# Attention pipeline of a two-stack transformer kernel: reciprocals one step later, weights in place, ScalarE copies between exponentials, compressed softmax spread over six steps

## What is computed

```python
def first_block(x, ...):
    for layer in range(DEPTH):                      # two layers
        h = rms_norm(x, attn_norm[layer])
        if layer % 2 == 0:                          # "layer 0"
            a_out = nsa_attention(...)              # compressed + selected + window branch, gated
            b_out = swa_sink_attention(...)         # sliding window with a sink
            x = x + jnp.concatenate([a_out, b_out], axis=-1) @ w_out_e[i]
        else:                                       # "layer 1"
            x = x + dilated_attention(...) @ w_out_o[j]
        x = x + (jax.nn.silu(gate) * up) @ w_down[layer]

def second_block(x, mem, ...):
    for layer in range(DEPTH):
        y = fox_shortconv_mixer(...) if layer % 2 == 0 else rglru_mixer(...)  # the first has a
        ...                                                # forgetting attention, 8 heads
        y = memory_cross_attention(h, m, ...)       # 4 heads of 256, 256 memory tokens
        ...
        y = swiglu(h, w_ffn_gu[layer], w_ffn_down[layer])

# each attention, per head and block of 128 queries:
s = q @ k.T * scale + mask;  p = softmax(s);  out = p @ v
```

## Time and profile before

| | |
|---|---|
| Runs | 3107.08, 3118.51, 3129.29 us; median 3118.51 |
| The profiled execution | 3109.32 us, of which 3107.5 us are the span from first to last instruction |
| Granted TensorE clock, mean | 0.958 |
| Busy share | PE 91%, DVE 36%, ACT 35%, POOL 42% |
| Chain that ended last | PE 81%, DVE 11%, ACT 4%, issue 3% |

### The profile page before, as it was taken

The page is one execution under the profiler, slowest core; times in us unless marked ns, Lnnn a source line. Parts: engine busy times, 40 slices in busy tenths (PEclk is TensorE's granted clock), DMA queues, the critical chain, the costliest instruction groups (busy, mean ns, idle before and its releaser), DMA issues.

```text
span 3107.5 us, 37798 instructions
## 1 busy us (share of the span) xinstructions
PE 2832.7 (91%) x13318; PEld 2229.3 (72%) x13318; DVE 1122.2 (36%) x1969; ACT 1089.1 (35%) x1761; POOL 1315.0 (42%) x691
## 2 busy tenths in 40 slices
PE   7977999999978999989988998999978689799997
PEld 5745788887746788867757876888856577588885
DVE  5554322112553322033446325221074573432202
ACT  5654322223654322232243333222225343332221
POOL 4544444444464444434344533444423364244442
PEclk9999999999999999989989998999988899899998
DMA  4300322333201333322203311223312231122331
GB/s 153 109 2 15 95 91 92 96 103 95 94 1 58 95 94 94 98 78 82 88 21 95 115 55 61 91 91 102 101 47 75 81 123 54 54 95 94 94 97 59
DMA packets 69090, 251.77 MB, mean 81 GB/s; under 512 B 7672, under 2 KB 7928, under 8 KB 68736
## 3 DMA queue, kind: packets, MB, share of 16 engines
q1 hardware_dynamic: 67104, 244.35, 24.9%
q10 hardware_dynamic: 1888, 6.14, 0.5%
HBM read 248.36 MB, written 2.10 MB: 81 GB/s over the span
## 4 chain that ended last, share of the span: by engine, by line
PE 81%; DVE 11%; ACT 4%; issue 3%; DMA 0%; ACTq 0%; POOL 0%; DVEq 0%; POOLq 0%
PE ps L512 25%; PE ps L513 24%; PE ps L514 24%; PE ps L622 3%; ACT pr L949 2%; PE ps L607 2%; PE ps L637 1%; DVE acc L1229 1%; DVE xl L1236 1%; DVE rstd L1250 1%; ACT pt L958 1%; DVE x L1509 1%; DVE y_mid L1508 1%; PE ps L578 1%; DVE u_r L1633 1%
## 5 line engine op out<-in xcount | busy, mean ns | idle before, releaser
L449 POOL TENSOR_TENSOR w_lo<-w_raw,w_hi 128x1024 fp32r<-128x1024 f32 x462 | 1117.5, 2422 | 1559.1 <-ACT w_hi L894 1549.6
L512 PE MATMUL ps<-xh,w_hi 128*128 128x512 f32 x2384 | 969.5, 407 | 85.3 <-DVE xl L1236 74.4
L513 PE MATMUL ps<-xl,w_hi 128*128 128x512 f32 x2384 | 960.2, 403 | 0.0
L514 PE MATMUL ps<-xh,w_lo 128*128 128x512 f32 x2384 | 945.4, 397 | 0.0
L894 ACT ACTIVATE w_hi<-w_raw 128x1024 fp32r<-128x1024 f32 x462 | 485.0, 1053 | 590.4 <-PE ps L514 589.7
L512 PEld LDWEIGHTS ps<-xh,w_hi 128*128 128x128 f32 x2384 | 451.8, 190 | 230.8 <-issue 70.6
L514 PEld LDWEIGHTS ps<-xh,w_lo 128*128 128x128 f32 x2384 | 454.4, 191 | 114.4
L513 PEld LDWEIGHTS ps<-xl,w_hi 128*128 128x128 f32 x2384 | 454.3, 191 | 103.1 <-issue 2.9
L512 PE MATMUL ps<-hh,w_hi 128*128 128x512 f32 x704 | 278.4, 396 | 0.0
L513 PE MATMUL ps<-hl,w_hi 128*128 128x512 f32 x704 | 278.4, 396 | 0.0
L514 PE MATMUL ps<-hh,w_lo 128*128 128x512 f32 x704 | 278.4, 395 | 0.0
(11 more groups left out here) (234 smaller groups left out, 2928.6 us busy)
## 6 DMA issues: line engine op xcount, KB each, us to landing
w_raw<-weights_in SPq DMA_DIRECT2D x462, 512.0 KB, 3.5
x<-x_in ACTq DMA_DIRECT2D x4, 512.0 KB, 10.1
mem<-mem_in ACTq DMA_DIRECT2D x2, 1024.0 KB, 4.9
x_out<-x SPq DMA_DIRECT2D x4, 512.0 KB, 2.6
rope<-rope_in ACTq DMA_DIRECT2D x1, 512.0 KB, 11.9
tab<-tables_in ACTq DMA_DIRECT2D x2, 256.0 KB, 2.8
tab<-tables_in ACTq DMA_DIRECT2D x1, 384.0 KB, 12.2
small<-small_in ACTq DMA_DIRECT2D x1, 326.5 KB, 4.7
```

Source lines behind the costliest of these rows:

```text
L449: nc.gpsimd.tensor_tensor(w_lo[:, slot], w_raw[:, slot], w_hi.bitcast(f32)[:, slot], ALU.subtract).then_inc(lo_ready, 1)
L512: nc.tensor.matmul(dst, w_hi[:, slot, w], hi, start=first, stop=False)
L513: nc.tensor.matmul(dst, w_hi[:, slot, w], lo, start=False, stop=False)
L514: return nc.tensor.matmul(dst, w_lo[:, slot, w], hi, start=False, stop=last)
```

## The change

In all five stretches:

- `sm` is gone. VectorE writes the masked scores straight into `pr`, which now has eight buffers; exponential and scaling work in place. VectorE waits for the transposes of the step four before (`n - 7`), the exponential for no transposes.
- VectorE's reciprocal of step s moves from the end of its round s to the end of its round s+1.
- Transposes of step s come in TensorE's round s+3 and ahead of the values, which come in round s+4; before, 2 and 3. `pt` has four buffers.
- ScalarE's copy stands between the two exponentials of its round.

In U0 the compressed softmax is spread out: scores in round s, mask and maximum in s+1, exponential in s+2, sum and weights in s+3, transposes in s+4, copy in s+5, with two buffers `s_c` and a semaphore for each stage. The third and fourth start at steps 14 and 26 in place of 15 and 28. The load of `cmask` is issued by ScalarE later, after the first root, and no longer belongs to the loads that TensorE waits for at the start. Four small tensors get other places in SBUF. No instruction of arithmetic is added or removed.

```diff
-        LAG = 3
+        TURN, LAG = 3, 4
-        CMP_STEPS = [(3, 0), (0, 2), (2, 15), (1, 28)]
+        CMP_STEPS = [(3, 0), (0, 2), (2, 14), (1, 26)]
...
-        sm = place("sm", [P, 4, T], 64)
-        pr = place("pr", [P, 4, T], 72)
-        pt = place("pt", [P, 3, T], 80)
+        pr = place("pr", [P, 8, T], 64)
+        pt = place("pt", [P, 4, T], 80)
...
 TensorE, after the scores of step s, ahead of the values:
+                    if TURN <= s < len(steps) + TURN:
+                        for a, u in enumerate(steps[s - TURN]["two"]):
+                            n = 2 * (s0 + s - TURN) + a
+                            pe.wait_ge(pn_ready, n + 1)
+                            if n >= 2:
+                                pe.wait_ge(pt_copied[a], n // 2)
+                            for kb in range(u["nk"] // P):
+                                last = nc.tensor.transpose(ps[:, PT_BANKS[a], tokens(kb)],
+                                                           pr[:, n % 8, tokens(kb)], ident[:])
+                            last.then_inc(pt_ready, 1)
...
 ScalarE:
-                        if n >= 4:
-                            act.wait_ge(pt_ready, n - 3)
-                        A(pr[:, n % 4, 0:nk], sm[:, n % 4, 0:nk], ACT.Exp, scale=-1.0,
-                          bias=negm[:, slot, a:a + 1],
-                          accum_out=den[:, slot, a:a + 1]).then_inc(p_ready, 1)
...
+                    if s < len(steps):
+                        exponential(0)
+                    if TURN <= s < len(steps) + TURN:
+                        copy_turned()
+                    if s < len(steps):
+                        exponential(1)
...
 VectorE:
-                        if n >= 4:
-                            dve.wait_ge(p_ready, n - 3)
+                        if n >= 8:
+                            dve.wait_ge(pt_ready, n - 7)
...
-                    if s < len(steps):
-                        dve.wait_ge(p_ready, 2 * (s0 + s) + 2)
-                        V.reciprocal(wgt[:, slot], den[:, slot]).then_inc(wgt_ready, 1)
+                    if 1 <= s <= len(steps):
+                        dve.wait_ge(p_ready, 2 * (s0 + s))
+                        before = (slot - 1) % 4
+                        V.reciprocal(wgt[:, before], den[:, before]).then_inc(wgt_ready, 1)
...
 Hooks of the compressed branch, TensorE, ScalarE, VectorE:
-                hooks.setdefault(s + 2, []).append(cmp_transposes(i))
+                hooks.setdefault(s + 4, []).append(cmp_transposes(i))
-                hooks.setdefault(s + 2, []).append(lambda i=i: cmp_copy(i))
-                hooks.setdefault(s, []).append(lambda i=i: cmp_exp(i))
+                hooks.setdefault(s + 2, []).append(lambda i=i: cmp_exp(i))
+                hooks.setdefault(s + 5, []).append(lambda i=i: cmp_copy(i))
-                hooks.setdefault(s + 1, []).append(lambda i=i, t=t: cmp_weights(i, t))
-                hooks.setdefault(s, []).append(lambda i=i, t=t: cmp_scores(i, t))
+                hooks.setdefault(s + 3, []).append(lambda i=i, t=t: cmp_weights(i, t))
+                hooks.setdefault(s + 1, []).append(lambda i=i, t=t: cmp_scores(i, t))
```

More of the change, by code:

```diff
@@ L35 @@
 ATANH_TERMS = 9
-CONST_DMAS = 4
+CONST_DMAS = 3
 X_TOTAL = 7 * KT
@@ L131, in two_stacks @@
         rstd = sb("rstd", [P, T])
+        with ExitStack() as over_acc:
+            hid, kc_t, cmask = (over_acc.enter_context(nc.sbuf_tensor(name, shape, f32)) for name, shape in
+                                (("hid", [P, 2, 2, BLK]), ("kc_t", [P, 2, 32]), ("cmask", [P, TB, 32])))
+        with nc.sbuf_tensor("gate_t", [P, TB, 24], f32) as gate_t:
+            pass
         acc = sb("acc", [P, T])
@@ L168, in two_stacks @@
         pc_t = place("pc_t", [P, 2, 2, P], 2)
-        s_c = place("s_c", [P, 8, 32], 4)
+        s_c = place("s_c", [P, 2, 8, 32], 4)
         z_v0 = place("z_v0", [P, 3, T], 4)
@@ L629, in attention @@
                         last.then_inc(o_done, 1)
[L630 to L639, removed]
                     for hook in hooks.get(s, []):
@@ L721, in run @@
                                                 kc_t[:].rearrange("p g c -> p (g c)"), start=True, stop=True)
-                    last.then_inc(cmp_ps, 1)
+                    last.then_inc(cmp_scored, 1)
                 return run
@@ L727, in run @@
                     pe.wait_ge(cmp_norm, i + 1)
+                    if i:
+                        pe.wait_ge(cmp_copied, i)
+                    else:
+                        pe.wait_ge(cmp_masked, 2)
                     for g in range(2):
@@ L942, in attention, with exponential, copy_turned @@
                 for s in range(len(steps) + LAG):
-                    for a, u in enumerate(steps[s]["two"] if s < len(steps) else []):
-                        n, slot = 2 * (s0 + s) + a, (s0 + s) % 4
-                        nk = u["nk"] + (u["sink"] is not None)
+                    slot = (s0 + s) % 4
+                    def exponential(a):
+                        u, n = steps[s]["two"][a], 2 * (s0 + s) + a
+                        p = pr[:, n % 8, 0:u["nk"] + (u["sink"] is not None)]
                         act.wait_ge(sm_done, n + 1)
-                        if n >= 4:
-                            act.wait_ge(pt_ready, n - 3)
-                        A(pr[:, n % 4, 0:nk], sm[:, n % 4, 0:nk], ACT.Exp, scale=-1.0,
-                          bias=negm[:, slot, a:a + 1],
-                          accum_out=den[:, slot, a:a + 1]).then_inc(p_ready, 1)
[L952 to L958, removed]
+                        A(p, p, ACT.Exp, scale=-1.0, bias=negm[:, slot, a:a + 1],
+                          accum_out=den[:, slot, a:a + 1]).then_inc(p_ready, 1)
+                    def copy_turned():
+                        n = 2 * (s0 + s - TURN) + 1
+                        nk = steps[s - TURN]["two"][1]["nk"]
+                        act.wait_ge(pt_ready, n + 1)
+                        if n >= 4:
+                            act.wait_ge(o_done, (n - 3) // 2)
+                        A(pt[:, n % 4, 0:nk], ps[:, PT_BANKS[1], 0:nk], ACT.Copy).then_inc(pt_copied[1], 1)
+                    if s < len(steps):
[4 more added lines that the diff above has]
+                        exponential(1)
                     if s >= LAG and steps[s - LAG]["ends"]:
@@ L1018, in _ @@
                     root()
+                    act.dma_start(cmask[:], cmpmask_in).then_inc(cmask_in, 16)
                 if m in (10, 14):
```

64 lines of the change are left out of this document (33 added, 31 removed).

## The result

The changed kernel takes **3040.35 us** (median of four runs, 3038.09 to 3042.11), the kernel before in the same series 3114.16. The ratio is 0.9759, 95% interval 0.9727 to 0.9791. A second series gave 3041.14 against 3107.43, ratio 0.9781 (0.9768 to 0.9794). The profiled execution took 3041.29 us (span 3039.5), against 3109.32 before: 68 us less, where the sum of the prediction had 49.

What follows compares the result with a forecast made beforehand. A one-round ring of waits, exponentials on transposes, idles TensorE; cut, TensorE binds. Terms 19.8 + 21.5 + 3 + 4.6 = 49 us off 3109.3 give 3060, or 3069.5 from the median; 3066 taken, range 3042 to 3100.

Steps and rivals of the forecast that it cites:

- The ring is cut: U1: exponentials stop waiting for transposes (36.7 us); TensorE then binds at 4.6 us per pair of rounds instead of 5.90.
- the closed ring: Rival: a three-round ring through transposes, copy, exponential and GpSimd holds the round at 2.95 us; 3112 to 3118; chance 0.08.
- half the gain: Rival: GpSimd waits for the late reciprocal and TensorE for GpSimd, a pair takes 5.3 us; 26 us, 3089; chance 0.22.
- The thin margin of the late reciprocal: Transposes in round s+3 come some 0.3 us after GpSimd's scaling ends, so the reciprocal may wait a round.
- U1, 19.8 us: TensorE idling in U1 falls from 27.8 us by 19.8; 8 stay: start 5, end 1, eight splits 2.
- U0, 21.5 us: TensorE idling in U0 falls from 41.5 us by 21.5; 20 stay.
- fill 8, end and splits 4, compressed branch 8: U0's 20 us of remaining TensorE idling: pipeline start, last copy with group splits, and VectorE's compressed work for four blocks.
- UF, 3 us: TensorE idling in UF falls from 8.1 us by 3, from trailing-round holes and tenths per pair; 5 stay.
- more than the sum: Rival: UF leaves the lower clock level earlier (up to 10 us) and fills shrink; 3045; chance 0.08.
- UX, 4.6 us: The two UX together lose 4.6 us as trailing rounds lose their holes, less one copy at the end.
- The clock as a loss: Rival: U1 and the rest of UF run at the lower clock, +40 us in all, 3149; chance 0.05.
- The instructions that GpSimd lengthens: U0: eight compressed-softmax instructions slowed beside GpSimd scaling cost 1.5 us, within the branch's 8; bounds nothing to 6 us.

Runs made afterwards that it cites:

- bufs_only: Kernel before with only the eight pr buffers and in-place exponential and scaling; 3071.68 us, ratio 0.9882 to the kernel before.
- bufs_lag: Changed kernel with the reciprocal back in its own round and ScalarE's copy back behind both exponentials; 3051.87 us, ratio 0.9807 to the kernel before.
- turn2_lag3: Changed kernel with transposes two and values three rounds after the scores in U1, UF and UX, U0 unchanged; 3079.59 us, ratio 0.9889 to the kernel before.
- cmp_old: Changed kernel with the compressed softmax staged as before, its blocks at steps 2, 15 and 28 again; 3042.45 us, ratio 0.9788 to the kernel before.
- recip_own: Changed kernel with only the reciprocal back at the end of its own round; 3052.68 us, ratio 0.9815 to the kernel before.

## Why the prediction was right or wrong

The sign and the mechanism were right, the size was not: I had put 3066 us as the median, 3042 to 3100 as the range, and 3040.35 were measured. Between the two profiled executions the sum was 19 us short. The other 6 us of the miss are what I had added to 3060 for the spread of the runs.

**The ring is cut: right.** Exponentials no longer wait for transposes, TensorE binds in U1 at 4.46 us a pair, 4.8 as the mean of the four pairs with splits among them (rounds 8 to 15, 19.4 us; forecast 4.6 to 4.8), and the rivals of the closed ring and of half the gain did not come. `bufs_only` says what the prediction did not: cutting this ring alone gives about half, since a second one, values behind the copy of their block, holds most of the rest: the later rounds give about 20 us (`bufs_lag`), reciprocal and copy together the last 10. The prediction had both in its chain but counted them as one.

**The thin margin of the late reciprocal: right.** Rounds s+3 are needed, as `turn2_lag3` shows with 20.1 us of waits for GpSimd.

**U1, 19.8 us: right**, 18.5 measured. Of the 8 that were to stay 8.9 did. But the parts were off: the start has 2.5 us of holes, not 5, and the splits have the other 4.6 of the 7.1 us, not 2.

**U0, 21.5 us: the failed step**, 33.2 measured. The prediction let 20 us of idling stay: fill 8, end and splits 4, compressed branch 8. 11.5 stayed: the terms for the fill and for the branch were too large. TensorE's waits in U0:

```profile
PE ps L611 <- DVE negm L1326: 6.3, 8, 2.0
...
PE ps L726 <- DVE s_c L1466: 1.5, 1, 1.5
...
PE ps L751 <- ACT pc_t L1075: 1.0, 1, 1.0
```

With 0.9 us at the compressed transposes (L739) the compressed branch holds 3.4 us, not 8. The splits with the first minima hold 6.3. The first ten us, where I had put a fill of 8, have 2.0 us of holes, 1.5 of which are the compressed branch's. So the fill is the larger error. The kernel before had shown less than 8 there already, 4.6 us of holes in its first twelve:

```profile
146.64 2.08 PE L607 MATMUL ps<-k_r,q_r 64*128 64x512 f32 x4 [3.28 <-DVE negm L1309]
...
152.34 1.10 PE L720 MATMUL ps<-kc_t,q_p 128*128 128x64 f32 x8 [1.29 <-ACT pc_t L1058]
```

And in U1, where I had put 5, it had 3.0. In the new order TensorE has one more round of scores to do before the first transposes, which start in U0 at 147.18 and in U1 at 829.16 without a wait for GpSimd. The mistake with the branch was to charge VectorE's 3.3 us per block as if VectorE were the bound, while the same argument had TensorE bind: VectorE waits for scores for 24.4 us in U0, and extra work falls into that. `cmp_old` shows it is not the spread that saves it: staged as before, U0 is as long at full clock. The other 3 us of U0's gain are not idle time at all but busy time, 111.4 to 108.3, which the sum never held. The lower clock is part of that: U0 had 11.5 us at 0.50 before and 6.8 after, worth at most 2.4 us.

**UF, 3 us: right as idle time, wrong as length.** Idling fell by 3.3 us (6.7 to 3.4), in the second pair of profiles from 6.6 to 3.0. The length fell by 9.7 (second pair 8.6), the rest being TensorE's busy time, 58.5 to 52.1: the spell at 1.2 GHz was 10 and 17 us in place of 24. This is the rival "more than the sum", which I gave 0.08, with its mechanism (UF leaves the lower level earlier) and nearly its size. It should have had more, since that row already stood there with 12 us to win and only idle time was counted.

**UX, 4.6 us:** 5.4 measured. The trailing rounds have no hole left.

**The clock as a loss:** refuted for this kernel as a whole; U1 did fall from 0.97 to 0.93, 11.5 us at the lower level in place of 6.8, which is worth at most 2.4 us that the forecast of U1 did not hold. Why a spell ends sooner in one kernel than in another stays open. Density alone does not explain it: the changed kernel and `recip_own` have the same order of work on TensorE and nearly the same idling in UF (3 and 2.4 us), but spells of 10 and 17 against 27 us; `turn2_lag3`, whose TensorE waits more, has 34. For the rule on transposes in the Trainium skill, "TensorE: Matmul & The Clock Gate", section "Part 4: PE-mode transpose", UF speaks neither way, as every variant has the same transposes.

**The instructions that GpSimd lengthens: about right.** One compressed instruction still takes 0.81 us beside a GpSimd scaling (143.58 to 145.09):

```profile
144.55 0.81 DVE L1466 TENSOR_TENSOR s_c<-s_c,cst 128x256 f32<-128x256 f32 x1
```

Its four take 424 to 810 ns with a median of 616, the other four (L1477) never over 426. That is 0.8 us in all, against the 1.5 taken, since only three of the eight fell on a scaling of GpSimd's, which is busy for 64.9 of U0's 119.8 us. Two of the three were lengthened; beside the third, VectorE's took its usual 0.42 us and GpSimd's 0.94 in place of 0.67. The rule of the Trainium skill, "SBUF — State Buffer", section "SBUF: two separate sides", that whichever of the two starts first keeps the other out for its whole instruction, had made it 9 us by the prediction's estimate; the trace shows waits of VectorE of at most 0.38. At 144.55 GpSimd's instruction had 0.54 us to go, so by these rows not even what was left of it was waited out, though spans on GpSimd are rough.

Had the sum counted the waits on VectorE only where TensorE cannot do without it, U0 would have stood at some 30, and 3109 - 58 is 3051. Of the last 10 us, 6.4 are busy time of UF that the longer spell at the lower clock had cost, and 3 are busy time of U0, in part the clock's; the rest are small terms of either sign.

## What to carry to other kernels

When the bound moves to another engine, work on the old one stops costing what it costs now: charge it only where the new bound waits for it. A ring seen in a chain of waits can be two rings of nearly equal length; cutting one shows the other, so price each with the other gone. Once a pipeline is full, look for the rare item in it (here the split of a finished group, placed ahead of the minima): moving it behind gave 8.4 us, and 67 us less work on GpSimd (197 to 130 over the five stretches) gave 3.4. And size the fill of a new order by the holes that the old one has there.

## What the hardware showed beyond that

GpSimd scales by two operands faster than by one. In the changed kernel, by form (count | busy, mean ns):

```profile
L490 POOL TENSOR_SCALAR pr<-pr,wgt 128x512 f32<-128x512 f32 x24 | 37.2, 1563 | 29.7 <-DVE wgt L1340 29.7
L492 POOL TENSOR_SCALAR pr<-pr,wgt,gate_t 128x512 f32<-128x512 f32 x16 | 12.1, 767 | 14.5 <-DVE wgt L1340 14.5
```

and with a column of ones as second operand

```profile
L490 POOL TENSOR_SCALAR pr<-pr,wgt,ones 128x512 f32<-128x512 f32 x24 | 18.2, 767 | 35.1 <-DVE wgt L1340 35.1
```

The column of ones halves the time of long rows and saves less on short ones: 1563 to 767 ns at 512 elements, 1242 to 661 at 384, 921 to 554 at 256, 602 to 448 at 128. Why is not shown. The other surprise is the spell at the lower clock, which within one stretch of unchanged arithmetic lasted from 10 to 34 us in thirteen profiles, starting 3 to 4 us into UF each time. What ends it is open.
